# Output projections of local and forgetting attention: half of the weight's rows by seven block products instead of eight

## The reference, cut to what matters

```python
def _swa_branch(x, w_in, sinks, w_out):
    ...
    return (o * jax.nn.silu(gate)) @ w_out          # (512, 1024) @ (1024, 1024)

def _fox_branch(x, w_in, b_f, w_out):
    ...
    o = _dense_causal(q, k, v, FOX_HEAD_DIM ** -0.5, cum).reshape(B, S, W)
    return (o * jax.nn.silu(gate)) @ w_out

def second_block(...):
    for i in range(DEPTH_2):
        ...
        x = _layernorm(DEEPNORM_ALPHA * x + y, ln_g[i], ln_b[i])
```

## Time and profile before

| what | value |
|---|---|
| runs | 1786.71, 1786.05, 1785.99 us; median 1786.05 |
| the profiled execution's own time | 1786.31 us |
| its span, first to last instruction | 1784.5 us |
| granted clock, mean | 0.998 |
| PE busy | 1763.0 us, 99% |
| DVE busy | 992.6 us, 56% |
| ACT busy | 810.8 us, 45% |
| POOL busy | 727.3 us, 41% |
| chain that ended last | PE 89%, DVE 7%, ACT 3%, issue 1% |

### The profile page before, as it was taken

The page is one execution under the profiler, slowest core; times in us unless marked ns, Lnnn a source line. Parts: engine busy times, 40 slices in busy tenths (PEclk is TensorE's granted clock), DMA queues, the critical chain, the costliest instruction groups (busy, mean ns, idle before and its releaser), DMA issues.

```text
span 1784.5 us, 24874 instructions
## 1 busy us (share of the span) xinstructions
PE 1763.0 (99%) x9776; PEld 1416.5 (79%) x9776; DVE 992.6 (56%) x2091; ACT 810.8 (45%) x1737; POOL 727.3 (41%) x441
## 2 busy tenths in 40 slices
PE   9999999999999999999999999999999999999997
PEld 6787877788888888889776798888877777887676
DVE  4558688564351524254777368755644342567764
ACT  5434455453342323244476344554345343446662
POOL 4534521154686868633312333234332324332122
PEclk9999999999999999999999999999999999999999
DMA  5322320153505151324212232113331222421212
GB/s 170 99 74 71 95 60 25 36 177 92 169 25 176 36 165 48 97 74 105 61 35 82 85 99 71 60 62 96 104 87 56 74 69 84 104 68 37 61 55 72
DMA packets 215032, 147.94 MB, mean 83 GB/s; under 512 B 51825, under 2 KB 197249, under 8 KB 214914
## 3 DMA queue, kind: packets, MB, share of 16 engines
q1 hardware_dynamic: 210592, 137.10, 27.2%
q10 hardware_dynamic: 4322, 9.24, 1.5%
HBM read 144.22 MB, written 2.10 MB: 82 GB/s over the span
## 4 chain that ended last, share of the span: by engine, by line
PE 89%; DVE 7%; ACT 3%; issue 1%; DMA 0%; POOL 0%; SPq 0%; DVEq 0%; ACTq 0%
PE PS L427 24%; PE PS L429 23%; PE PS L428 23%; PE PS L515 6%; PE PS L577 6%; PE PS L601 4%; PE PS L779 1%; DVE PS L1645 1%; ACT X L1172 1%; DVE X L1648 1%; DVE PS L1664 1%; PE PS L1033 1%; PE PS L802 1%; ACT Wh L1113 0%; PE PS L1054 0%
## 5 line engine op out<-in xcount | busy, mean ns | idle before, releaser
L2291 POOL TENSOR_TENSOR Wl<-Wr,Wh 128x1024 fp32r<-128x1024 f32 (+3 forms) x367 | 600.9, 1657 | 1005.4 <-ACT Wh L1113 1005.1
L427 PE MATMUL PS<-XTl,Wh 128*128 128x512 f32 (+1 forms) x1096 | 412.9, 377 | 1.0 <-DVE KF L1683 0.8
L429 PE MATMUL PS<-XTh,Wh 128*128 128x512 f32 (+1 forms) x1096 | 408.1, 372 | 0.0
L428 PE MATMUL PS<-XTh,Wl 128*128 128x512 f32 (+1 forms) x1096 | 408.0, 372 | 0.0
L1113 ACT CAST Wh<-Wr 128x1024 fp32r<-128x1024 f32 (+5 forms) x274 | 249.3, 931 | 156.9 <-PE PS L429 95.7
L427 PEld LDWEIGHTS PS<-XTl,Wh 128*128 128x128 f32 x1096 | 206.5, 188 | 45.5 <-issue 9.9
L429 PEld LDWEIGHTS PS<-XTh,Wh 128*128 128x128 f32 x1096 | 206.4, 188 | 36.4
L428 PEld LDWEIGHTS PS<-XTh,Wl 128*128 128x128 f32 x1096 | 206.5, 188 | 34.8
L427 PE MATMUL PS<-Wl,XTh 128*128 128x512 f32 (+2 forms) x608 | 227.3, 374 | 2.1 <-DVE XTl L1656 1.5
L429 PE MATMUL PS<-Wh,XTh 128*128 128x512 f32 (+2 forms) x608 | 224.1, 369 | 0.0
L428 PE MATMUL PS<-Wh,XTl 128*128 128x512 f32 (+2 forms) x608 | 223.9, 368 | 0.0
(11 more groups left out here) (342 smaller groups left out, 2749.5 us busy)
## 6 DMA issues: line engine op xcount, KB each, us to landing
Wr<-in_w_in SPq DMA_DIRECT2D x38, 512.0 KB, 3.8
Wr<-in_fox_w_in SPq DMA_DIRECT2D x32, 512.0 KB, 4.2
Wr<-in_w_ffn_gate SPq DMA_DIRECT2D x22, 512.0 KB, 4.2
Wr<-in_w_ffn_up SPq DMA_DIRECT2D x22, 512.0 KB, 4.0
Wr<-in_swa_w_in SPq DMA_DIRECT2D x20, 512.0 KB, 4.0
WP<-in_w_ffn_down SPq DMA_DIRECT2D x9, 1024.0 KB, 9.2
Wr<-in_mla_w_in SPq DMA_DIRECT2D x16, 512.0 KB, 4.2
Wr<-in_mla_w_out SPq DMA_DIRECT2D x16, 512.0 KB, 3.4
```

What stands on the lines that cost most here:

```text
L427: pe.matmul(o, l[0], r[1], start=start, stop=False, skip_group_check=again)
L428: pe.matmul(o, l[1], r[0], start=False, stop=False, skip_group_check=again)
L429: return pe.matmul(o, l[0], r[0], start=False, stop=stop, skip_group_check=again)
L2291: ins = raw.tensor_tensor(l[:, cs], r[:, cs], h[:, cs].bitcast(F), sub)
```

## The change

In local and forgetting attention (`SEVENS`) row tiles 0 to 3 of the output weight are taken as two pairs, and each pair (2 row tiles x 2 column halves) is multiplied with its 2 x 2 blocks of the gated values (2 row tiles x 2 token halves of 256) by seven block products of two products each. The results are combined on PSUM and `X`; row tiles 4 to 7 then add on as before.

- PE (`outproj7`): for each pair an "even" piece and a "sums" piece, eight products; then an "odd" piece for each pair and one "fours" piece for both, six products a pair; then rows 4 to 7. Before the second part it waits for DVE's `combine` to have read each bank.
- Pieces: seven for rows 0 to 3 instead of four. An odd row tile is also loaded a second time, for the sums alone.
- POOL (`sums7`): four additions of 128 x 512 a pair, in front of the remainder of that pair's even piece. In local attention those of pair 0 wait for the factors of pair 1.
- DVE and ACT (`factors`): differences, high and low parts of the left factors, at gates 2 and 4 of local and at gates 3 and 5 of forgetting attention. The "out" steps of rows 0 to 3 go.
- DVE (`combine`): twelve operations in front of the layer's tail. The residual's factor goes to 1.0 for six of eight tiles, since `combine` has applied it.
- `due` of `("fu", 21)` is two higher. This touches the feed-forward's last projection.

```diff
+SEVENS = {'swa': (2, 4), 'fox': (3, 5)}
...
-                    due[signal, key] = min(count[0] + AHEAD + (key[:2] == ("swa", 1)), len(used) + W_SLOTS)
+                    due[signal, key] = min(count[0] + AHEAD + (key[:2] == ("swa", 1)) + 2 * (key == ("fu", 21)), len(used) + W_SLOTS)
...
+            def outproj7(s, src, lhs, ready, turned=True):
...
+                for q in range(2):
+                    w2 = weight(row(2 * q), D, ("even", s, q))
+                    odd_src[w2] = row(2 * q + 1)
+                    w13 = weight(row(2 * q), D, ("sums", s, q))
+                    for bs, w, h, j, x in ((A, w2, 0, 0, "A"), (B, w2, 1, 5, "B"), (C, w13, 0, 4, "C"), (E, w13, 1, 3, "E")):
+                        for v in range(2):
+                            ins = product(bs, v, w, h, j, q, q == 0, q == 1)
+                            if q:
+                                ins.then_inc(*done(psum_full, "part", s, x, v))
...
+                for q in range(2):
+                    wo = weight(row(2 * q + 1), D, ("odd", s, q))
+                    if q == 0:
+                        w4 = weight(row(0), D, ("fours", s, 0))
+                    for bs, w, h, j, x in ((A, wo, 0, 1, "A"), (C, wo, 1, 6, "C"), (E, w4, q, 2, "E")):
+                        for v in range(2):
+                            e.wait_ge(by_dve.at("part", s, x, v))
+                            ins = product(bs, v, w, h, j, q, False, False, again=True)
...
+                ws = [(weight(row(a), D), a) for a in range(4, 8)]
+                for i in range(NT):
+                    for c in range(2):
+                        b, fresh = place[i, c], i >= 2 and c == 1
...
-            outproj(s, by_rows(A["swa_w_out_2"][0]), XT, lambda a: [by_dve.at("swa", "out", a)])
+            outproj7(s, by_rows(A["swa_w_out_2"][0]), XT, lambda a: [by_dve.at("swa", "out", a)])
...
+            def factors(s, q):
+
+                FS, _, _, S4 = O7[s]
+                g = GT[s][:, 2 * q:2 * q + 2, :].rearrange("p f (a t) -> p (f a) t", a=2)
+                e.wait_ge(by_dve.at(s, "o", 2 * q + 1), *overlaid(s, q))
+                high(FS[0][:, q, 0, :], g[:, 0, :], "fs_hi", s, q)
+                high(FS[0][:, q, 1:3, :], g[:, 2:4, :], "fs_hi", s, q)
+                e.wait_ge(by_dve.at("sf", s, q))
+                high(FS[0][:, q, 3:7, :], S4[:, :, :], "fs_hi", s, q)
...
+            def combine(s):
+
+                for x in "ACEB":
+                    for v in range(2):
...
+                        e.wait_ge(psum_full.at("part", s, x, v), by_dve.now())
+                        if x in "AB":
+                            scale = ALPHA if x == "A" else 1.0
+                            ve.scalar_tensor_tensor(low, low, scale, b, mult, add).then_inc(*by_dve.next())
+                            ve.scalar_tensor_tensor(right, right, scale, b.unsqueeze(1).broadcast_to([128, 2, 512]), mult, sub).then_inc(*by_dve.next("part", s, x, v))
+                        else:
+                            y = X[:, v + 2, HALVES[1]]
+                            ve.tensor_tensor(y, y, b, add if x == "C" else sub).then_inc(*by_dve.next("part", s, x, v))
...
+            def factors(s, q):
...
+                ve.tensor_tensor(S4[:, 0, :], g[:, 0, :], g[:, 1, :], sub).then_inc(*by_dve.next())
+                ve.tensor_tensor(S4[:, 1, :], g[:, 1, :], g[:, 3, :], sub).then_inc(*by_dve.next())
+                e.wait_ge(by_dve.now())
+                ve.tensor_tensor(S4[:, 2, :], S4[:, 1, :], g[:, 0, :], sub).then_inc(*by_dve.next())
+                e.wait_ge(by_dve.now())
+                ve.tensor_tensor(S4[:, 3, :], S4[:, 2, :], g[:, 2, :], add).then_inc(*by_dve.next("sf", s, q))
+                e.wait_ge(by_act.at("fs_hi", s, q), by_dve.now())
+                low(FS[1][:, q, 0, :], g[:, 0, :], FS[0][:, q, 0, :], "fs", s, q)
+                low(FS[1][:, q, 1:3, :], g[:, 2:4, :], FS[0][:, q, 1:3, :], "fs", s, q)
+                low(FS[1][:, q, 3:7, :], S4[:, :, :], FS[0][:, q, 3:7, :], "fs", s, q)
...
-                    elif kind == "out":
+                        if x in SEVENS.get(s, ()):
+                            factors(s, SEVENS[s].index(x))
+                    elif kind == "out" and (x >= 4 or s not in SEVENS):
                         gated(s, x)
...
+            def sums7(i, s, q):
+
+                slots = [ring[x] % RAW_SLOTS for x in (i, ("odd", i))]
+                w, o = (Wr[x] for x in slots)
+                t, f = O7[s][1][:, :, :].rearrange("p (a b) n -> p a (b n)", a=2), O7[s][2]
+                e.wait_ge(raw_in[slots[0]].at(i), raw_in[slots[1]].at("odd", i), *([weight_lo.at(at_home["sums", s, 0])] if q else [by_dve.at("fs", s, 1)] if s == "swa" else []))
+                raw.tensor_tensor(t[:, 0, :], w[:, HALVES[0]], w[:, HALVES[1]], add).then_inc(*by_pool.next())
+                raw.tensor_tensor(t[:, 1, :], w[:, HALVES[1]], o[:, HALVES[1]], add).then_inc(*by_pool.next("sums", s, q))
+                e.wait_ge(by_pool.now())
+                raw.tensor_tensor(w[:, HALVES[1]], t[:, 0, :], o[:, HALVES[1]], add).then_inc(*by_pool.next("even", s, q))
+                e.wait_ge(by_pool.now())
+                raw.tensor_tensor(f[:, q, :], w[:, HALVES[1]], o[:, HALVES[0]], add).then_inc(*by_pool.next("fours", s, q))
```

More of the change, by code:

```diff
@@ L1091, in tensor @@
                     give(b, (by_dve, (s, "o", x)))
[L1092 removed]
+            outproj7(s, by_rows(A["fox_w_out_2"][0]), XT, lambda a: [by_dve.at("fox", "out", a)])
             mla(1)
@@ L1547, in scalar @@
                             *by_act.next("turned", s, x, u, 0))
-                elif kind == "out":
+                elif kind == "gate" and x in SEVENS.get(s, ()):
+                    factors(s, SEVENS[s].index(x))
+                elif kind == "out" and (x >= 4 or s not in SEVENS):
                     gated(s, x)
```

108 lines of the change are left out of this document (90 added, 18 removed).

## The result

The changed kernel takes **1801.05 us** (median of 4 runs, 1800.79 to 1801.69) where the kernel before, beside it, takes 1786.38 (1785.99 to 1787.24): a ratio of 1.0079, 95% interval [1.0067, 1.0092]. It is 14.7 us slower; 1801.0 was forecast.

A forecast was written before the change was run, and what follows sets the result against it. PE, 99% busy at 2.4 GHz, was taken as the bound, with other engines level in local attention. Feed-forward -2.35, local attention +13.9 and forgetting attention +3.2 gave +14.7 on 1786.3: 1801 us, range 1785 to 1807.

The forecast's parts named there:

- -2.35: Feed-forward's last projection: the later due time shortens PE's start-to-start of 2.58 us to 0.23, a gain of 2.35 us.
- +1.45: Local attention, gate 2: the serial factors delay pair 3's copies to 1137.5, so PE loses 1.45 us.
- +12.5: Local attention: GpSimd's late remainder and sums delay VectorE's scalings; PE turns pair 7 at 1196.7, not 1184.23, 12.5 us later.
- behind that remainder now come the sums of pair 1: three of them between the last four scalings, 4.05 us: Local attention, pair 7: the old collision stays and three sums between VectorE's last four scalings add 4.05 us.
- 8.4 us late: Local attention, pair 6: remainder rest 1.6, four sums 5.4 and 1.4 earlier lateness make the scaling end at 1178.5, not 1170.04.
- over 8 us long in all: Sign in the trace after: with four sums between them, VectorE's scalings of pair 6 last over 8 us in all.
- +0.4: Local attention, gate 4: the factor chain ends pair 5's copies at 1168.5, 0.4 us late for PE, counted within +12.5.
- two copies (0.56 each) to 1137.5; PE wanted them at 1136.11: Local attention behind gate 2: end of the serial factor chain, VectorE's copies of pair 3, giving PE's +1.45 us.
- A rival with 0.15: Clock falls to 1.2 GHz in PE's stop before turn 7, slowing turn 7 and gate job 7: +5.4, 1806 us; chance 0.15.
- the rival of half the collisions: VectorE slips several scalings between two sums: 5.7 us on pair 6, none on pair 7; +6.7, 1793 us; chance 0.22.
- Of the 2.7 us nothing is left: Each projection: four products less save 2.7 us, but GpSimd's eleven remainders for eight make weight rows 6 and 7 late.
- VectorE's work on SBUF operands: Shared port: a GpSimd instruction stops this work for its whole length; PSUM copies and gates run on.

The follow-up runs named there:

- experiment 1: Kernel before with only the later due time of the feed-forward's weight row ("fu", 21): 1783.73 us against 1787.04, ratio 0.9982.
- experiment 12: Kernel before with only the later due time of ("fu", 21), measured a second time: 1783.47 us against 1787.17, ratio 0.9982.
- experiment 4: Changed kernel with GpSimd's four sums in local attention cut to 8 columns each: 1793.65 us against 1787.04 for the kernel before, ratio 1.0037.
- experiment 6: Changed kernel with the second half of local attention's factors moved behind the next pair's scalings: 1796.82 us against 1786.16 for the kernel before, ratio 1.0060.
- experiment 9: Changed kernel with seven products in forgetting attention alone, VectorE making low parts of rows 4, 6 and 7: 1784.99 us against 1786.15 for the kernel before.
- Experiment 7: Changed kernel with the fourth weight piece due one later in both attentions' projections: 1798.21 us against 1786.16 for the kernel before, ratio 1.0065.
- experiment 8: Changed kernel with seven products in forgetting attention alone and its fourth weight piece due one later: 1787.6 us against 1786.16 for the kernel before.
- experiment 2: Changed kernel with seven products in forgetting attention alone, local attention's projection plain: 1786.78 us against 1787.04 for the kernel before, ratio 1.0001.
- experiment 3: Changed kernel with seven products in local attention alone: 1797.4 us against 1787.04 for the kernel before, ratio 1.0055.
- experiment 5: Changed kernel with local attention's factors at gates 1 and 3 instead of 2 and 4: 1806.33 us against 1786.16 for the kernel before, ratio 1.0111.

## Why the prediction was right, point by point

**The total** was met to 0.05 us, and that is partly luck. By the traces VectorE's lateness up to turn 7 was put 2.9 us too high, and the clock, 4.5 us, was not in the sum; the two errors nearly cancel. The traces themselves differ by 15.4 us, the medians by 14.7.

**Feed-forward.** -2.35 forecast, -2.5 measured, and kept to the end (experiments 1 and 12).

**Local attention up to turn 7.** Forecast +1.45 and +12.5, so 13.95; measured 11.0, all of it VectorE's: its last scaling ends at 1192.34. The mechanism was the forecast's: sums and scalings alternate one for one on the port, as four scalings in 5.16 us and experiment 4 show. Its sizes were off. The largest error is the step "behind that remainder now come the sums of pair 1: three of them between the last four scalings, 4.05 us": there were two, 2.0 us more than before, since only three scalings follow the remainder and the first of them slipped in ahead of the first sum. Inside the "8.4 us late" of pair 6 (measured 7.7) three errors partly cancel: the copies behind gate 4 were 2.4 us late and not 1.4, the rest of the remainder cost 1.2 and not 1.6, and the four sums cost 4.0 and not 5.4. So the scalings of pair 6 were not "over 8 us long in all" but 6.6, and the "+0.4" of PE at gate 4 was 1.5, as at gate 2.

**Where the factors bite.** The step "two copies (0.56 each) to 1137.5; PE wanted them at 1136.11" has the right size, but the stop is at another place. PE stops before the score, not before value 3: on ScalarE the query's copy (1132.29) stands behind the third high part and a weight's rounding. I had costed the factors on VectorE and on ScalarE as one serial chain and not asked what else was queued on ScalarE. VectorE's chain was as late all the same: its copies end at 1134.56, and without the stop before the score value 3 would have wanted them at 1133.25 (1136.11 less the shift of 2.86), so PE would have stood 1.3 us there. Experiment 6 takes both away and doesn't separate them.

**The clock.** A rival with 0.15, "from a stop of 8 us before turn 7", 5.4 us. It did fall, three times, after much shorter stops, and cost 4.5 us: 2.8 behind turn 7, 1.75 in the projection, where the rival did not look for it, and nothing behind turn 6. So the rival's mechanism is part of the truth: without it the change would have cost about 10 us, between the forecast and the rival of half the collisions (+6.7). By the Trainium skill (TensorE: Matmul & The Clock Gate, What's actually happening) the clock drops after idleness; the windows agree, at 0.76, 0.56 and 0.71. I should have carried the fall with a chance at each of the new stops, not only at one of 8 us.

**The projections.** Local: +0.4 forecast, +0.3 measured without the clock (waits of 1.3 and 1.5 us against the 2.7 saved), +2.05 with it. Forgetting: +1.0 at T0 forecast, +0.5 measured; +2.2 in the projection forecast, +2.4 measured; the fourth weight is rounded at T0 + 5.8, forecast T0 + 5.75. PE has a third stop there, of 1.3 us, for the remainder of the fourth piece (1509.91 to 1511.22). "Of the 2.7 us nothing is left" holds in both. Its cause, eleven remainders for eight, is borne out by experiment 9, which takes three out of GpSimd's row and leaves 0.5 us of the waits at rows 6 and 7. Experiment 7 takes out one: one of the four waits goes. For forgetting attention the forecast had named the link from remainder to low parts to gate 7 to table load; experiment 8 shows it at work.

**The port.** By the Trainium skill (SBUF — State Buffer, Who interferes with whom) whoever is first holds the shared pair for its whole instruction. The rows agree from both sides: 3.40 us for GpSimd's remainder behind VectorE's 1.22, and 1.39 us for a VectorE addition of four columns behind GpSimd. The forecast's "VectorE's work on SBUF operands" was too wide. The reciprocal at 1169.44, which reads one SBUF operand of four columns, ran beside a sum in its usual 0.18 us; what was held up in these rows are the scalings and the instructions with two SBUF operands.

**Combining on VectorE** was costed at nothing; in local attention PE is busy for all of 1204.00 to 1224.50, the products before row 6, and in forgetting attention its one stop before row 6 is for GpSimd.

What stays open: why the clock fell after some stops and not after others (last section), and whether some other order of local attention's steps would free VectorE of its lag; placing the factors at gates 2 and 3 was not tried.

## What to carry to other kernels

A saving on the busiest engine counts only if the engines behind it can pay for it. Here 5.4 us of products asked for 22 more GpSimd instructions, 44 of VectorE and 10 of ScalarE, in stages where VectorE was level with TensorE. Where GpSimd has a row of instructions queued and VectorE a row of scalings or of operations on two SBUF operands, price each short VectorE instruction at one whole GpSimd instruction, and follow the lag to the next stage's table loads and roundings. Ask of each delay which engine sets the next common point: the first fall of the clock lay in the shadow of VectorE and cost nothing. Look also at the small line beside the large one: a due time changed by two pieces gained 2.5 us, and no version of the algebra tried here gained anything on top of it.

## What the runs showed of the hardware that was not expected

The clock does not follow the length of the last stops. All versions have one stop of 1.70 us from start to start near 1100 us. In the kernel before the clock stayed at 1.00 behind it, in the traces of experiments 2, 3 and 9 it fell for 3.4 us. Windows of before and of experiment 2:

```profile
1099.00:1106.00 7.00, 5.63 (x55) 4.25 (x54) 4.84 (x8) 4.44 (x10) 4.68 (x2) 1.00 0.43 123
```

```profile
1099.00:1106.00 7.00, 5.64 (x41) 4.32 (x39) 5.82 (x13) 2.91 (x5) 4.67 (x2) 0.76 0.49 135
```

In forgetting attention's projection 1.69 and 1.80 us brought it down in experiment 2 (the window there), while 1.68 and 1.80 in experiment 6 and 1.72 and 2.05 in the changed kernel left it at 1.00. It also stayed at 1.00 behind a stop of 2.58 us in the kernel before, and behind 2.28 us before turn 7 in experiment 4; it fell behind 1.03 and 2.20 us close together at turn 6, and behind 3.67 to 4.85 before turn 7. About the same stops, two outcomes: an estimate should carry the fall with a chance, not a threshold. Once it had fallen it stayed low for 3.4, 6.8 or (experiment 5) 10.2 us, in the changed kernel with PE busy in all of the three windows shown.

A VectorE instruction on four columns, 0.15 us by itself, lasted 1.39 us behind a remainder of GpSimd (1168.02) and 1.96 in experiment 5 (1120.63): its small size did not protect it.
